# Unnormalised keys and queries in the recurrent heads of a two-layer hybrid encoder: their lengths enter as columns

## The reference

```python
q, k, v = split(silu(causal_dwconv(concat([q, k, v]), conv_w)))
q = l2norm(q) * DN_DK ** -0.5                 # l2norm(t) = t * rsqrt(sum(t*t) + 1e-6), per token
k = l2norm(k)
beta = sigmoid(b);  g = -exp(a_log) * softplus(a + dt_bias);  G = cumsum(g) in a chunk
m = tril(beta_i * (k_i . k_j) * exp(G_i - G_j), -1) + I
u, w = solve(m, [beta * v, beta * exp(G) * k])
for each chunk:
    v_new = u - w @ state
    o = (q * exp(G)) @ state + (tril(q_i . k_j * exp(G_i - G_j))) @ v_new
    state = state * exp(G_last) + (k * exp(G_last - G)).T @ v_new
o = o * rsqrt(mean(o * o) + 1e-6) * norm_w * silu(z)
```

## Time and profile before

| | us |
|---|---|
| median of three runs | 3166.64 |
| the three runs | 3166.64, 3166.77, 3164.72 |
| span of the profiled execution | 3165.2 |
| PE busy | 3110.6 (98%) |
| PE weight loads busy | 2593.9 (82%) |
| DVE busy | 1471.4 (46%) |
| ACT busy | 720.8 (23%) |
| POOL busy | 1736.3 (55%) |

### The profile page before, as it was taken

The page is one execution under the profiler, slowest core; times in us unless marked ns, Lnnn a source line. Parts: engine busy times, 40 slices in busy tenths (PEclk is TensorE's granted clock), DMA queues, the critical chain, the costliest instruction groups (busy, mean ns, idle before and its releaser), DMA issues.

```text
span 3165.2 us, 42772 instructions
## 1 busy us (share of the span) xinstructions
PE 3110.6 (98%) x15968; PEld 2593.9 (82%) x15968; DVE 1471.4 (46%) x2202; ACT 720.8 (23%) x1433; POOL 1736.3 (55%) x987
## 2 busy tenths in 40 slices
PE   8999999999999999999999999999999999999998
PEld 7888875788888979888888888667888889788887
DVE  3332367755536336332244314677555472353323
ACT  1110224422221423110121103134222224231102
POOL 6666553433346745666656665535333567456664
PEclk9999999999999999999999999999999999999999
DMA  4323221211122322333322332212111224222332
GB/s 155 99 94 106 97 94 40 74 54 54 57 83 87 127 74 87 93 99 100 100 91 96 99 100 92 92 41 74 61 54 51 86 90 130 70 86 94 99 100 67
DMA packets 81173, 272.79 MB, mean 86 GB/s; under 512 B 8433, under 2 KB 16913, under 8 KB 81041
## 3 DMA queue, kind: packets, MB, share of 16 engines
q1 hardware_dynamic: 75808, 264.27, 25.7%
q10 hardware_dynamic: 5088, 5.96, 0.6%
q0 software_dynamic: 144, 0.66, 0.1%
HBM read 268.73 MB, written 2.12 MB: 86 GB/s over the span
## 4 chain that ended last, share of the span: by engine, by line
PE 94%; DVE 3%; ACT 1%; issue 1%; DMA 0%; SPq 0%; ACTq 0%; DVEq 0%
PE acc L618 82%; PE aux L618 12%; PE aux L879 1%; DVE xf L1819 0%; DVE xl L1735 0%; DVE xf L1816 0%; DMA xf<-in_xT 0%; DVE ml L1735 0%; ACT xf L1321 0%; PE aux L1249 0%; DVE xf L1760 0%; DVE y_sum L1774 0%; ACT tmp L1321 0%; ACT xh L1321 0%; DVE lr L2056 0%
## 5 line engine op out<-in xcount | busy, mean ns | idle before, releaser
L589 POOL TENSOR_TENSOR wl<-raw,wh 128x1024 fp32r<-128x1024 f32 x496 | 1213.8, 2449 | 80.1 <-ACT wh L1321 40.1
L592 POOL TENSOR_SCALAR wh<-raw 128x1024 fp32r<-128x1024 f32 x480 | 523.3, 1090 | 1314.2 <-PE acc L618 901.0
L618 PE MATMUL acc<-xh,wh 128*128 128x512 f32 (+1 forms) x2688 | 1016.8, 383 | 17.9 <-ACT xh L1321 15.1
L618 PE MATMUL acc<-xh,wl 128*128 128x512 f32 (+1 forms) x2688 | 987.2, 372 | 0.0
L618 PE MATMUL acc<-xl,wh 128*128 128x512 f32 (+1 forms) x2688 | 948.2, 371 | 0.0
L618 PEld LDWEIGHTS acc<-xh,wh 128*128 128x128 f32 x2688 | 512.9, 191 | 127.0 <-issue 38.7
L618 PEld LDWEIGHTS acc<-xh,wl 128*128 128x128 f32 x2688 | 513.4, 191 | 79.1 <-issue 1.9
L618 PEld LDWEIGHTS acc<-xl,wh 128*128 128x128 f32 x2688 | 488.2, 190 | 87.8
L1735 DVE TENSOR_TENSOR hl<-tmp,hh 128x512 f32 x88 | 238.4, 2709 | 81.8 <-ACT hh L1321 81.8
L618 PE MATMUL acc<-hl,wh 128*128 128x512 f32 (+1 forms) x704 | 264.5, 376 | 0.0
L618 PE MATMUL acc<-hh,wl 128*128 128x512 f32 (+1 forms) x704 | 264.5, 376 | 0.0
(11 more groups left out here) (287 smaller groups left out, 3912.6 us busy)
## 6 DMA issues: line engine op xcount, KB each, us to landing
raw<-in_stream SPq DMA_DIRECT2D x496, 512.0 KB, 3.3
xf<-in_xT SPq DMA_DIRECT2D x2, 1024.0 KB, 10.5
bias<-rel_scratch ACTq DMA_DIRECT2D x2, 1024.0 KB, 6.0
mraw<-in_memT ACTq DMA_DIRECT2D x2, 1024.0 KB, 5.8
out_xT<-xf SPq DMA_DIRECT2D x16, 128.0 KB, 1.7
gate_w<-in_gate_w ACTq DMA_DIRECT2D x2, 512.0 KB, 5.5
const<-in_const POOLq DMA_DIRECT2D x1, 640.0 KB, 6.6
sc<-in_ba_w ACTq DMA_DIRECT2D x2, 256.0 KB, 5.7
```

Source lines behind the costliest of these rows:

```text
L589: pool.tensor_tensor(wl[:, s, :], raw[:, s, :], wh[:, s, :].bitcast(F32), ALU.subtract).then_inc(unit_split, 1)
L592: pool.tensor_scalar(wh[:, s, :], raw[:, s, :], 1.0, 0.0, ALU.mult, ALU.add).then_inc(hi_step, 1)
L618: return pe.matmul(out, w, x, start=start, stop=stop, skip_group_check=True)
```

## The change

Keys and queries stay as they are after silu. `k_spread`, `q_spread`, `k_normed` and `q_normed` are gone, with the waits that stood in front of them. The sums of squares are handled as columns of 4 values per partition: `k_rate` = beta / (sum of squares + eps) takes the place of beta in the rows of the system (`m`) and in `vn`; `v_scale`, the root of the sum, becomes the scale of the values in `vk` (4 ACT instructions, one for each 128 tokens, instead of one); the queries' sum goes into the argument of the output's root (`o_arg`). For the columns DVE has five small instructions more at s = 4 (`o_arg`, `k_sum`, `q_sum`, `k_inv`, `k_rate`), all after `t4` of the running head, and ACT one more. ACT's root `v_scale` now waits for DVE's `k_sum`, and `std` for `o_arg`, where both read PE's result before. For head 0, `kk` moves ahead of `norm_cols`, behind a wait for `silu1`, and the parts of FILL_AHEAD are dealt out anew.

```diff
 LRU_DRAIN = {0: 20, 1: 24, 3: 28}
-FILL_AHEAD = {(0, "norm_cols"): 10, (0, "k_spread"): 4, (0, "q_spread"): 2, (0, "kk"): 2, (0, "k_turned"): 2,
+FILL_AHEAD = {(0, "kk"): 6, (0, "norm_cols"): 6, (0, "k_turned"): 6,
               (HN - 1, "rms_cols"): 2, (HN - 1, "o_spread"): 2}
...
 def pe_beside(s, n, p):
-    return {1: only(n, "decay_rows"), 4: only(p, "rms_cols") + only(n, "norm_cols"), 5: only(n, "k_spread"),
-            6: only(n, "q_spread")}.get(s, [])
+    return {1: only(n, "decay_rows"), 4: only(p, "rms_cols") + (only(0, "kk") if n == 0 else []) + only(n, "norm_cols")}.get(s, [])
...
                         if n < HN:
-                            filled(n, "norm_cols")
+                            if n:
+                                filled(n, "norm_cols")
                             act(n, "exp_g")
...
                             squares_summed(p)
+                        if n == 0:
+                            dve(0, "silu1")
+                            keys_by_keys(0)
                         if n < HN:
+                            if n == 0:
+                                filled(n, "norm_cols")
                             act(n, "sq1")
...
                             done(columns(1, sq_sum[:, :]), n, "norm_cols")
-                    if s == 5 and n < HN:
-                        dve(n - 1, "rate")
-                        spread(n, 0, "k_spread")
-                    if s == 6 and n < HN:
-                        if p >= 0:
-                            dve(p, "o_normed")
-                        else:
-                            dve(n, "k_normed")
-                        spread(n, 1, "q_spread")
+
+                def columns_read(n):
+
+                    dve(n, "q_sum")
...
                     beside(s, 0, -1)
-                keys_by_keys(0)
                 keys_turned(0)
...
                         act(h - 1, "o_sq")
-                    dve(h, "q_normed")
+                    else:
+                        columns_read(0)
+                    dve(h, "silu0")
                     for c in range(CH):
...
                             if h + 1 < HN:
-                                dve(h + 1, "k_normed")
-                            else:
-                                dve(h, "rate")
-                            spread(h - 1, 2, "o_spread")
+                                columns_read(h + 1)
+                            dve(h - 1, "rate")
+                            out_spread(h - 1)
                         filled(h, f"p{s}")
...
                     if h + 1 < HN:
-                        dve(h + 1, "k_normed")
+                        dve(h + 1, "silu1")
                         keys_by_keys(h + 1)
...
                         filled(h, f"o{c}")
-                        if c == 0 and h + 1 < HN:
-                            dve(h + 1, "q_normed")
-                        elif c == 0 and h:
+                        if c == 0 and h:
                             dve(h - 1, "o_normed")
+                        elif c == 0:
+                            columns_read(1)
                         dve(h, f"v{c}")
...
-                def roots(a, b, step):
-                    done(fn(rates[:, a:b, :], B5[:, a * CH:b * CH].rearrange("p (x c) -> p x c", c=CH), ACT.Sqrt, bias=eps_l2[:, :]),
-                         step, "std")
+                def value_scale(n):
+                    drain(l, filled_before(n, "norm_cols"))
+                    dve(n, "k_sum")
+                    done(fn(v_scale2[n % 2][:, :], k_sum[:, :], ACT.Sqrt, scale=0.25, bias=eps_0[:, :]), n, "v_scale")
+
+                def out_root(p):
+                    drain(l, filled_before(p, "rms_cols"))
+                    dve(p, "o_arg")
+                    done(fn(o_rate[:, :], o_rate[:, :], ACT.Sqrt, bias=eps_q[:, :]), p, "std")
...
                         if n < HN:
-                            pe_(n, "norm_cols")
-                        else:
-                            pe_(p, "rms_cols")
-                        roots(0 if n < HN else 2, 3 if p >= 0 else 2, n - 1)
+                            value_scale(n)
+                        if p >= 0:
+                            out_root(p)
                         if n < HN:
...
                     pe_(h, "v_turned")
-                    done(fn(vk[:, :, :], tiles(B6), ACT.Copy, scale=0.5), h, "vk")
+                    for c in range(CH):
+                        last = fn(vk[:, c, :], tiles(B6)[:, c, :], ACT.Identity, scale=v_scale2[h % 2][:, c:c + 1],
+                                  bias=eps_0[:, :])
+                    done(last, h, "vk")
                     pe_(h, "inv0_turned")
...
-                def inverse_roots(a, b, step):
-                    act_(step, "std")
-                    done(dve.reciprocal(rates[:, a:b, :], rates[:, a:b, :]), step, "rate")
+                def out_arg(p):
+                    pe_(p, "rms_cols")
+                    done(stt_(o_rate[:, :], q_sum3[p % 3][:, :], Q_EPS, B5[:, 2 * CH:3 * CH], ALU.mult, ALU.add), p, "o_arg")
+
+                def key_rate(n):
+                    pe_(n, "norm_cols")
+                    done(ts_(k_sum[:, :], B5[:, 0:CH], 4 * NORM_EPS, None, ALU.add), n, "k_sum")
+                    done(dve.tensor_copy(q_sum3[n % 3][:, :], B5[:, CH:2 * CH]), n, "q_sum")
+                    own(n, "k_sum")
+                    done(dve.reciprocal(k_rate2[n % 2][:, :], k_sum[:, :]), n, "k_inv")
+                    own(n, "k_inv")
+                    k_rate = k_rate2[n % 2].rearrange("p (c a) -> p c a", a=1)
+                    done(tt_(k_rate, k_rate, cols[:, 1, :, n:n + 1], ALU.mult), n, "k_rate")
+
+                def out_rate(p):
+                    act_(p, "std")
+                    done(dve.reciprocal(o_rate[:, :], o_rate[:, :]), p, "rate")
...
                     if s == 4:
-                        drain(l, filled_before(n, "norm_cols") if n < HN else filled_before(p, "rms_cols"))
-                        inverse_roots(0 if n < HN else 2, 3 if p >= 0 else 2, n - 1)
+                        if p >= 0:
+                            out_arg(p)
+                        if n < HN:
+                            key_rate(n)
+                        if p >= 0:
+                            out_rate(p)
                         if n == 0:
...
                         if n < HN:
-                            pe_(n, "k_spread")
-                            done(tt_(dc[:, 1, :], dc[:, 1, :], B5, ALU.mult), n, "k_normed")
                             silu_of(n, 2)
...
                             head_out(p)
-                        if n < HN:
-                            pe_(n, "q_spread")
-                            done(stt_(dc[:, 0, :], dc[:, 0, :], float(P) ** -0.5, B5, ALU.mult, ALU.mult), n, "q_normed")
...
                     own(n, "decay")
+                    own(n, "k_rate")
                     pe_(n, "kk")
                     for c in range(CH):
-                        last = stt_(mt[:, c, :], tiles(B4)[:, c, :], cols[:, 1, c, n:n + 1], dt_[:, c, :], ALU.mult, ALU.mult)
+                        last = stt_(mt[:, c, :], tiles(B4)[:, c, :], k_rate2[n % 2][:, c:c + 1], dt_[:, c, :], ALU.mult, ALU.mult)
                     done(last, n, "m")
```

More of the change, by code:

```diff
@@ L48 @@
 LRU_C = 8.0
+DK = 128
+Q_EPS = 4 * NORM_EPS * DK
 UNIT = 1024
@@ L296, in act_beside @@
     return {1: only(n, "exp_g", "th1"), 2: only(n, "decay_exp", "kd_exp", "last_exp", "sq1", "th0"), 3: only(n, "sq0"),
-            4: [(n - 1, "std")] + only(n, "th2") + only(p, "z_th")}.get(s, [])
+            4: only(n, "v_scale") + only(p, "std") + only(n, "th2") + only(p, "z_th")}.get(s, [])
 def act_core(h, beside):
@@ L315, in dve_beside @@
             2: only(n, "decay", "silu0") + (only(n, "conv2") if n else []),
-            4: [(n - 1, "rate")] + (only(0, "conv2") if n == 0 else []),
-            5: only(n, "k_normed", "silu2") + (only(1, "conv1") if n == 0 else []) + only(p, "z_gate"),
-            6: only(p, "o_normed", "y") + only(n, "q_normed")}.get(s, [])
+            4: only(p, "o_arg") + only(n, "k_sum", "q_sum", "k_inv", "k_rate") + only(p, "rate") + (only(0, "conv2") if n == 0 else []),
+            5: only(n, "silu2") + (only(1, "conv1") if n == 0 else []) + only(p, "z_gate"),
+            6: only(p, "o_normed", "y")}.get(s, [])
 DVE_LATE = (1, 2, 4)
@@ L335, in dve_tail @@
             + ahead[2:] + only(h, "v3"))
-DN_PE = delta_steps(lambda n: only(n, "kk", "k_turned"), pe_beside, pe_core, pe_tail, lambda p: only(p, "rms_cols", "o_spread"))
-DN_ACT = delta_steps(lambda n: only(n, "kg"), act_beside, act_core, act_tail, lambda p: [(HN, "std")] + only(p, "z_th", "y_hi"))
+DN_PE = delta_steps(lambda n: only(n, *(("kk",) if n else ()), "k_turned"), pe_beside, pe_core, pe_tail, lambda p: only(p, "rms_cols", "o_spread"))
+DN_ACT = delta_steps(lambda n: only(n, "kg"), act_beside, act_core, act_tail, lambda p: only(p, "std", "z_th", "y_hi"))
```

(34 more changed lines are left out.)

## The result

The changed kernel takes 3189.4 us (median of 4 runs, 3188.4 to 3192.9), the kernel before 3166.7 beside it: a ratio of 1.0075 [1.0062, 1.0088], 22.7 us slower. Forecast were 3177.6 and 3162 to 3187. The sign was right, the time lies outside the range, and half of the loss wasn't foreseen.

What follows compares the result with a forecast made beforehand. PE, busy 98% of the span, was taken as the bound. Per layer -6.5 - 1.4 - 0.8 + 5.5 + 1.6 + 5.5 + 1.6 = +5.5 us, +11 for both, giving 3177.6 us; range 3162 to 3187.

Steps and rivals of the forecast that it cites:

- The removed work: PE in the heads: 8 spreads a layer go, 128 records fewer in all; -6.5 us per layer.
- both old waits: Head 0: PE's waits for k_normed and the rates go, -0.6 and -0.8, in sum -1.4 us per layer.
- The old clock dip: PE's low clock behind norm_cols and a 0.6 us wait, 1.7 us lost; half taken as gone, -0.8 (0 to -1.7).
- The first new wait: Head 0 behind decay_rows: PE waits for exp_g, decay_min and silu1 with no parts between; 5.5 us per layer (4.5 to 8.2).
- The second new wait: Head 0 ahead of k_turned(0): PE waits for m, as POOL holds DVE; 5.5 us per layer (0.6 to 6.4).
- The clock behind it: Stretch at the low PE clock behind the wait ahead of k_turned(0); 1.6 us per layer (0 to 2.5).
- Heads 1 to 3: ACT's copy of p5 later, +0.2 us in each of two heads, against savings elsewhere; 0 taken for all (-0.7 to +6).
- the cut of parts shifts by two: Parts dealt for head 0 are 18, not 20; in heads 1 and 2 a gate tile's tanh falls before ACT's copy, 0.6.
- slower still: Rival: DVE k_sum, ACT v_scale, copy of p5 hold PE 1.5 us in each of heads 1 to 3; 3186.6 us, 12%.
- The rule on the shared port: POOL holds DVE instructions with two SBUF inputs or in two-port mode; so k_rate, convs and silu2 make the second wait long.
- slower: Outcome class: measured time over 3173.0 us; chance given as 0.60.
- same: Rival: DVE not held, the second wait does not form, 3164.7 us, 24%; as outcome class given 0.27.

Runs made afterwards that it cites:

- e1: Changed kernel with the 6 parts of kk(0) issued ahead of PE's waits for exp_g, decay_min and silu1; 3175.2 us, ratio 1.0029 to the kernel before.
- e3: Kernel before with 8 parts for norm_cols(0) in place of 10, so 18 for head 0; 3178.3 us, ratio 1.0043.
- e7: e4 with 8 parts in place of 10 for k_turned(0), a cut of 18; 3161.8 us, ratio 0.9987 to the kernel before.
- e4: Changed kernel with e1's edit and head 0's parts dealt kk 10, norm_cols 0, k_turned 10 (20 in sum); 3146.8 us, ratio 0.9938 to before.
- e6: Kernel before with POOL's low part cut to 64 of 1024 columns behind the first four units; 3141.7 us.
- e2: Changed kernel with 8 parts for k_turned(0) in place of 6, so 20 for head 0 as before; 3165.5 us, ratio 1.0001 to the kernel before.

## Why the prediction was right in sign and wrong in size

- **The removed work**: right. 128 records fewer, both old waits gone. The old clock dip, of which half was taken (-0.8), went whole (-1.7): between 621 and 647 us the granted clock is full, `norm_cols` at 635.43 included.
- **The first new wait**: 4.9 us a layer for 5.5, for the reason given (nothing between `decay_rows` and the waits, POOL silent, `y_lo` and `kd_arg` at their free durations). With its clock it is worth 7.1 a layer (e1), the forecast's 5.5 + 1.6; that these agree to the tenth is luck, as the wait was 0.6 short and the slow stretch behind it cost about 2.2 (615.9 to 620.3 at the low level).
- **The second new wait**: 5.3 for 5.5. The reading that a unit begins just behind `norm_cols` and that both convs are held was right. The clock behind it: `k_turned` and `v_turned` start 3.47 us apart (650.91 to 654.38) against 1.83 in the kernel before, 1.64 for the 1.6 taken. So both waits were followed by a slow stretch, as the Trainium skill (TensorE: Matmul & The Clock Gate, section "What's actually happening") led one to expect.
- **The balance of the preparation**: head 1's `decay_rows`, before p2, starts 6.2 us later, first before, then after:

```profile
655.23 1.12 PE L618 MATMUL aux<-rows,const 4*128 4x512 f32 x2
```

```profile
661.46 1.12 PE L623 MATMUL aux<-rows,const 4*128 4x512 f32 x2
```

By the forecast's terms: 10.4 us for all but the spreads of heads 1 to 3, less 2.8 for the two parts not issued yet, 7.6. What came was 1.4 less, mainly since the old dip went whole and the first gap was 0.6 shorter.
- **The failed step** is "Heads 1 to 3 ... I take 0 for all (-0.7 to +6)", with head 0's own levels, which it passed over. The text says itself that "the cut of parts shifts by two", and follows that shift only to a gate's tanh on ACT. It doesn't ask where POOL's pairs fall. In the profiled pair a layer grew by 12.9 us (half of 3191.0 - 3165.2): 6.2, 2.8 for the parts issued later, -4.9 for six spreads, and so 8.8 for the heads, where 0 stood. The cut alone costs 12.1 us in the kernel before (e3) and 15.0 in the covered one (e7 less e4), 6 to 7.5 a layer. In the profiled pair the waits for `n3` are 3.6 us a layer of the 8.8 (7.5 in place of 0.3 for both). The clock is the larger part: from head 1's `decay_rows` to 140 us behind head 3's, in both layers and summed over stretches of 2 us, it is at its low level for 34 us after and 10 us before, and 24 us at half speed are 12 us lost, 6 a layer. The two together make 9.6, a little over the 8.8; where the rest came back I did not follow. The size of the clock's part changes from one execution to another: e1, with the same waits for `n3`, has 20 us at the low level, and the profiled run of the kernel after is the slowest of its four. (By the medians of the runs, 22.7 instead of 25.8, the heads' share is 7.3 a layer.)
- **The rivals**: "slower still" had a price near the truth, by the wrong chain. ACT's chain through `v_scale` and the copy of p5 held nobody: PE's waits for ACT's `tmp` are 4.7 us in 6 times in both kernels. `vk` in four instructions took 1.51 us and was hidden, as said.
- **The rule on the shared port** (Trainium skill, GPSIMD Engine Reference, section Specifications) was used for one stretch, and the trace agrees there and in the heads: `decay` (L2085 and L2112), with two SBUF inputs, took 2.88 us beside POOL and 0.69 free. The conv's `tensor_scalar` reads one tensor from SBUF and was held too, 0.48 us free and 1.3 to 2.6 beside POOL; whether it runs in a two-port mode the trace doesn't show. The forecast applied it only where a wait was already under suspicion. One of the two rows that it took as evidence carries none: `m` at 644.02 met POOL's subtraction, over at 644.23, for 0.2 us only.
- **The range**: its upper end, 3187, was set by the ACT chain at 1.5 us a head. A bound for the heads from the convs' own rows (2.07 + 3.16 beside POOL against 0.43 + 2.32, 2.5 us in each of three places) would have reached past the result.
- **The chances**: the cases as stated add up to 0.57 for slower (0.9 x 50 + 12) and 0.30 for same (24 + 5 + 1), not 0.60 and 0.27. It changes nothing in the outcome.

## What to carry to other kernels

When background work is dealt out in parts, a changed number of parts at one place moves the phase of everything behind it: compare, for each later step, which engine starts what beside it, before and after, and not only at the place of the edit. A step that is taken forward on an engine with one ordered list must bring its cover with it; here the same change costs 0.75% without and brings 0.6 to 0.75% with cover and phase. A sweep of the phase over one period (here four parts, 18 us from best to worst) belongs to such a change.

## What the runs showed of the hardware

- A DVE instruction with its tensors in SBUF that meets POOL's 128x1024 subtraction waits it out: `decay` (L2085 at 618.87 in the kernel before) took 2.88 us where the same step took 0.69 free, and conv `tensor_scalar` 2.6 where it took 0.47. Beside POOL's shorter instruction for the high part (1.05 us) it was 1.3 for the conv, and 0.83 for `kd_arg`, which took 0.16 free. POOL's subtraction took 2.35 to 2.8 us in these stretches.
- POOL's long instruction costs the kernel before 25 us of 3167 in all (e6), though POOL appears nowhere in its chain.
- The granted clock fell to 1.2 GHz in the heads in two ways. In the kernel before it fell with no idle of PE at all, behind 24 records of one-column fp32 matmuls: 0.57 in the mean from 748 to 752. In the kernel after, with a wait of 1.55 us just ahead of the same matmuls, it stayed low for about 10 us: `ones,sq_sum` x8 took 1.84 us at 756.04, and 1.03 at 636.24 in the same kernel. In e2 the same matmuls (747.65 to 750.4) had no fall behind them, and the window from 740 to 765 shows 1.00; what decides between the two no run here shows.
